# A hybrid encoder on one Trainium2 core: the first two projection blocks of the attention layer change places

## The reference

```python
# layer 0: pooling mixer (not touched by the change)
h = rms_norm(x, pool_norm);  x = x + pool_mixer(h, ...)
# layer 1: dilated window attention, 3 groups (window, dilation), 8 heads of 128
h = rms_norm(x, att_norm)
proj = h @ w_in                      # 1024 x 10240: q, k, v for each of 3 groups, and a gate
for g in range(3):
    q = rotary(rms_norm(qkv[:, :, g, 0], q_norm[g]), pos, 32, theta)
    k = rotary(rms_norm(qkv[:, :, g, 1], k_norm[g]), pos, 32, theta)
    o, lse = dilated_window_attention(q, k, qkv[:, :, g, 2], dilation, side)
weights = softmax(lses over the groups)
x = x + ((sum of weights * outs) * silu(gate)) @ w_out
```

## Time and profile before

| | |
|---|---|
| median of 3 runs | 1763.33 us (1762.72 to 1766.46) |
| profiled execution | 1765.1 us, its span 1763.3 us |
| PE busy | 1698.2 us (96%), 8328 matmuls |
| DVE busy | 1134.4 us (64%) |
| ACT busy | 830.0 us (47%) |
| POOL busy | 264.7 us (15%) |
| mean granted TensorE clock | 0.987 |
| share of the last chain on PE | 73% |

### The profile page before, as it was taken

One profiled execution on the slowest core, in us unless ns is written; L12 is line 12 of the kernel. 1 busy time (PEld: TensorE's weight loads), 2 busy tenths in 40 slices (PEclk: granted clock), 3 DMA queues, 4 the chain that ended last, 5 costly groups with the idle time before them and its releaser, 6 DMA issues.

```text
span 1763.3 us, 23697 instructions
## 1 busy us (share of the span) xinstructions
PE 1698.2 (96%) x8328; PEld 1423.3 (81%) x8328; DVE 1134.4 (64%) x1900; ACT 830.0 (47%) x1944; POOL 264.7 (15%) x288
## 2 busy tenths in 40 slices
PE   6999999999999988999999999999999999989977
PEld 6878877788888776888888888888888899978866
DVE  5875667655665688735868357683575256577664
ACT  5543333322121364534655247463564378864542
POOL 3223333100000123201423014130131000000000
PEclk9999999999999999999999999999999999999989
DMA  5144232492322423342332523233245557666635
GB/s 182 49 133 130 96 96 96 156 344 88 128 72 72 140 72 118 122 143 72 120 112 80 173 79 123 81 119 117 76 160 197 184 174 256 220 211 226 211 110 175
DMA packets 143923, 242.98 MB, mean 138 GB/s; under 512 B 16448, under 2 KB 54336, under 8 KB 142784
## 3 DMA queue, kind: packets, MB, share of 16 engines
q1 hardware_dynamic: 138912, 224.18, 38.3%
q10 hardware_dynamic: 4896, 17.30, 2.8%
HBM read 161.69 MB, written 79.76 MB: 137 GB/s over the span
## 4 chain that ended last, share of the span: by engine, by line
PE 73%; DVE 5%; issue 2%; ACT 2%; POOL 1%; DMA 0%; SPq 0%; DVEq 0%; ACTq 0%; POOLq 0%
PE pair L965 20%; PE pair L967 20%; PE pair L966 20%; PE pair L1250 4%; PE pair L1221 4%; PE pair L1182 3%; PE pair L1230 2%; ACT both L2268 1%; POOL qrstd L957 0%; DMA both<-part_spill 0%; POOL qvar L952 0%; DVE both L1804 0%; DVE bufS L1546 0%; DVE bufU L1546 0%; DVE hTl L1819 0%
## 5 line engine op out<-in xcount | busy, mean ns | idle before, releaser
L965 PE MATMUL pair<-w,turnh 128*128 128x512 f32 x640 | 250.8, 392 | 10.6 <-ACT both L2147 4.9
L966 PE MATMUL pair<-w,turnh 128*128 128x512 f32 x640 | 250.5, 391 | 0.0
L967 PE MATMUL pair<-w,turnl 128*128 128x512 f32 x640 | 250.4, 391 | 0.0
L965 PE MATMUL pair<-w,hTh 128*128 128x512 f32 x608 | 241.3, 397 | 1.0 <-DVE xs L1336 0.8
L967 PE MATMUL pair<-w,hTl 128*128 128x512 f32 x608 | 238.1, 392 | 0.0
L966 PE MATMUL pair<-w,hTh 128*128 128x512 f32 x608 | 238.0, 392 | 0.0
L2147 ACT ACTIVATE both<-pair 128x512 f32<-128x512 f32 x160 | 93.7, 592 | 178.3 <-PE pair L967 164.0
L1698 DVE TENSOR_TENSOR both<-pair,both 128x512 f32<-128x512 f32 x120 | 81.7, 687 | 123.7 <-PE pair L967 121.5
L965 PEld LDWEIGHTS pair<-w,turnh 128*128 128x128 f32 x640 | 121.1, 189 | 37.3 <-issue 9.0
L2158 ACT ACTIVATE dump<-both 128x128 f32<-128x128 f32 x384 | 119.4, 311 | 63.4 <-DVE both L1698 50.8
L967 PEld LDWEIGHTS pair<-w,turnl 128*128 128x128 f32 x640 | 121.0, 189 | 25.3
(11 more groups left out here) (199 smaller groups left out, 3660.9 us busy)
## 6 DMA issues: line engine op xcount, KB each, us to landing
part_spill<-both SPq DMA_DIRECT2D x160, 256.0 KB, 3.6
both<-part_spill SPq DMA_DIRECT2D x22, 1024.0 KB, 6.8
raw_z<-in_att_w_in_dram SPq DMA_DIRECT2D x20, 1024.0 KB, 5.3
raw<-in_pool_w_in_dram SPq DMA_DIRECT2D x32, 512.0 KB, 5.4
raw<-in_att_w_in_dram SPq DMA_DIRECT2D x10, 1024.0 KB, 6.3
raw_u<-in_att_w_in_dram SPq DMA_DIRECT2D x10, 1024.0 KB, 6.0
diff_spill<-ubuf SPq DMA_DIRECT2D x16, 512.0 KB, 2.7
raw<-in_pool_w_out_dram SPq DMA_DIRECT2D x16, 512.0 KB, 4.4
```

The costliest lines, as they stand in the source:

```text
L965: nc.tensor.matmul(out, lh, rh, start=first, stop=False, skip_group_check=onto)
L966: nc.tensor.matmul(out, lh, rl, start=False, stop=False, skip_group_check=onto)
L967: return nc.tensor.matmul(out, ll, rh, start=False, stop=last, skip_group_check=onto)
```

## The change

`BLOCKS` has its first two items changed about: V0 is block 0 and K0 is block 1. Nothing else is edited; the lists of all engines follow from this tuple.

```diff
-    BLOCKS = ((K, 0), (V, 0), (Q, 0), (K, 1), (V, 1), (Q, 1), (K, 2), (G, 0), (Q, 2), (V, 2))
+    BLOCKS = ((V, 0), (K, 0), (Q, 0), (K, 1), (V, 1), (Q, 1), (K, 2), (G, 0), (Q, 2), (V, 2))
```

## The result

The changed kernel took 1753.28 us (median of 4 runs, 1750.94 to 1754.25) against 1763.03 us before (4 runs): a ratio of 0.9946, 95% interval 0.9933 to 0.996. Two later measurements of it, five runs each beside 21 and 15 of before, gave 1754.25 and 1755.03 us, ratios 0.9956 (0.9943 to 0.997) and 0.9957 (0.9944 to 0.9969). By the two larger measurements it is 7 to 8 us faster; the forecast was 1755.5, by a saving of 7.9. The first pair of medians differs by 9.8, more than the 6.9 to 8.9 that the forecast held likeliest.

A forecast was written before the change was run, and what follows sets the result against it. The prediction took PE to bound the kernel, with waits and slow clock only in block 0 of the projection. Terms of 0.94, 0.03, 2.34, 2.88 and 1.67 sum to 7.86 us, giving 1755.5 from 1763.3; range 1752.5 to 1760.0.

The forecast's parts named there:

- What bounds: PE bounds the kernel; only its gaps or slower clock matter, and in the projection only block 0 has them.
- The sum: Block 0, products 3 to 5: 0.94 + 0.03 + 2.34 + 2.88 + 1.67 = 7.86 us saved.
- 0.03, 2.34, 1.67 and 2.88: Savings in us: product 3's excess length, gap ahead of product 4, product 4's slow clock, gap ahead of product 5.
- Products 3, 4, 5: In block 0 their inputs would be ready 1.6, 3.8 and 1.2 us before PE, saving gaps of 0.94, 2.34 and 2.88.
- Rival 1: Product 5 in block 0 still waits: saving only 3.3 to 5 us, 1758.3 to 1760.0; chance 0.11.
- The clock: PE's slow stretch at 678 to 682, in product 4, disappears once PE runs unbroken: 1.67 us saved.
- rival 2: A slow clock stretch stays somewhere: saving 6.2 us, 1757.1; chance 0.08.
- the gap of 4.9: PE's 4.9 us wait for ACT's copies ahead of product 2 in block 0, forecast to stay with its slow stretch.
- Block 1 at 0: K0's squares, POOL operations, fold and rotations moved into block 1 cost 0 us, covered by DVE's 19 us left.
- Rivals 3 and 4: Idle handed on to block 1 or 2, 1761.5 to 1763.5, chance 0.07; three rotated blocks in a row, 1770.1, 0.04.

The follow-up runs named there:

- sum_first: Kernel before, K0 still first, with only the low half of the fourth token sum moved ahead of one rotation on DVE: 1759.24 us, ratio 0.9988.
- late_rot: Kernel before, K0 still first, with its fold and first eight rotations moved behind the fourth token sum on DVE: 1763.64 us, ratio 1.0007 to before.
- spread_rot: Kernel before, K0 still first, with fold and rotations behind the fourth token sum, one rotation at most parts: 1759.45 us, ratio 0.9985 to before.
- carry_rot: Kernel before, K0 still first, rotations spread behind the fourth token sum and the last four carried into V0: 1760.11 us, ratio 0.9987 to before.
- q_first: Kernel before with block order Q0, V0, K0, K1, so another rotated block is first: 1763.04 us, ratio 1.0002 to before.
- again_2: The changed kernel measured once more, with no further edit: 1755.03 us, ratio 0.9957 to before.
- six_in_row: Changed kernel reordered to V0, V1, K0, Q0, K1, Q1, K2, Q2, G, V2: 1754.00 us, ratio 0.9952 to the kernel before.

## Why the prediction was right

- *What bounds.* Right: nothing but block 0's waits and clock changed for PE, and in the changed kernel 735 of 735 us from 655 to 1390 are busy (before 729.3).
- *The sum.* 7.86 forecast; 8.09, 7.90 and 8.17 in three profiles, against one profile of before; 7 to 8 in the larger measurements. One term was slightly off: an undisturbed product takes 10.88 us (from 661.13 to 672.01, and again to 682.89), while the forecast took 10.95 from products 5 and 6 of the profile before. Over products 3 to 6 this makes 0.28 us, which is the difference between the forecast's 6.92 from product 3 on (0.03, 2.34, 1.67 and 2.88) and the measured 7.20. The median forecast, 1755.5, is 2.2 above the first measurement and within 1.3 of the two later ones. The first pair of medians alone (9.8) would have spoken for a larger saving than forecast; in the profiles the difference lies ahead of and behind the projection, in instructions that the change doesn't touch, and the later measurements do not repeat it; so I take it for chance and not for a missed term.
- *Products 3, 4, 5.* The margins came out at 1.7, 3.8 and 1.3 us (ends at 659.47, 668.21 and 681.61 in the DVE rows, starts at 661.13, 672.01 and 682.89); forecast were 1.6, 3.8 and 1.2. Rival 1 did not happen.
- *The clock.* The stretch near 678 is gone and none came elsewhere in the projection (rival 2 did not happen; the stretch behind the gap of 4.9 does differ from run to run, by up to 0.3 us in the three profiles of the changed kernel). The split of the sum was too sharp, as `sum_first` shows: in these two terms the clock and the gap behind it trade.
- *Block 1 at 0.* Shown by leaving the work out: 720.80 us from product 3 on with it and without it. Rivals 3 and 4 did not happen; six rotated blocks in a row cost nothing.
- *What the prediction gave as the reason* (rotations stood ahead of three instructions) is true but short. It would let one think that moving them a few places is enough. Block 0 has the three last `sum_low`, `fourth_sums` and `last_token_sum` on top of a block's work. Three later places for the rotations each made a new wait. Two things stood behind these: DVE had more to do without a pause than the time to the next product allows (all of it in `late_rot`), and DVE waited for ACT's splits, which stand behind squares that wait for DVE's additions (2.0 us in two waits in `spread_rot`, 5.0 in two in `carry_rot`). My expectations for all three were wrong in this. Leaving block 0 is what worked; an order that also uses DVE's idle time ahead of `sum_low(3)` stays untested.

## What to carry to other kernels

When work that exists once (here the token sums) shares a stretch with work that comes in some of the stages, let the stage without the extra work be the first: a swap of two list items was worth three times the best of the four re-orderings tried inside the stage. To price it, take the whole stretch against the same number of undisturbed units, not gap by gap, and lay out the engines anew with measured distances from start to start; margins came out within 0.1 us. Judge a saving of half a per cent by the distance between two places that enclose the edit, since the rest of the span scattered by several us; the distance that starts behind the last disturbed place agreed to 0.01 us over seven profiles. When work is moved behind one critical instruction, look for the next one behind it on the same engine, and for the idle time that it leaves.

## What was not expected of the hardware

- A gap is not always followed by a slow clock: 2.17 us of wait ahead of product 4 was followed by a slow product 4 before (12.39 us from first to last start), and by a full-speed one in `sum_first` (10.75) with 2.16. The 2.75 ahead of product 5 was punished in `q_first` and the 2.73 before was not.
- Behind the same wait of 4.9 us, in lists that are the same up to there, the slow stretch was of different length from run to run: 8 steps of about 0.43 us instead of 0.23 in `again_2` and `six_in_row`, 9 in before and after, 12 in `sum_first`. A longer one ahead of a wait shortens this wait, so that it shows in the time only where PE waits for nothing next.
